# Sigmoid gates of two branches computed beside their branch products, with eight places for the attention heads' outputs

## What is computed

```
xn   = rms_norm(x, norm1_g)
proj = xn @ w_in        # q/k/v of mixers A, B, C and gate_pre (3 x 1024 columns)
o_a = dilated window attention (3 groups, 6 heads)      # width 384
o_b = bidirectional mLSTM (4 heads)                      # width 512
o_c = differential attention (4 heads), rms norm per head  # width 512
gates = sigmoid(gate_pre)                                # (3, 1024) per token
mixed = gates0 * (o_a @ w_a) + gates1 * (o_b @ w_b) + gates2 * (o_c @ w_c)
x = x + mixed @ w_out
x = x + (silu(hg) * hu) @ w_ffn_out,  hg, hu = split(rms_norm(x, norm2_g) @ w_ffn_in)
```

## Time and profile before

| | us |
|---|---|
| median of 3 runs | 3378.49 (3377.2 to 3378.5) |
| the profiled execution | 3374.39 |
| its span, first to last instruction | 3372.8 |
| PE busy in the span | 3162.7 |
| DVE, ACT, POOL busy | 1559.9, 1172.6, 511.2 |
| mean granted TensorE clock | 0.983 |

### The profile page before, as it was taken

One profiled execution on the slowest core, in us unless ns is written; L12 is line 12 of the kernel. 1 busy time (PEld: TensorE's weight loads), 2 busy tenths in 40 slices (PEclk: granted clock), 3 DMA queues, 4 the chain that ended last, 5 costly groups with the idle time before them and its releaser, 6 DMA issues. The chain is left out here.

```text
span 3372.8 us, 45846 instructions
## 1 busy us (share of the span) xinstructions
PE 3162.7 (94%) x17652; PEld 2898.3 (86%) x17652; DVE 1559.9 (46%) x3181; ACT 1172.6 (35%) x2496; POOL 511.2 (15%) x879
## 2 busy tenths in 40 slices
PE   6899999899999999999988999999999999999998
PEld 6899988788787999999878998887887889999997
DVE  5445235654465343443464442457544653433433
ACT  4334434465532211111143344344655322111110
POOL 1111322122152000000001113212212510000000
PEclk9999999999999999999989999999999999999999
DMA  3434443443275221221133344434433842212211
GB/s 129 142 113 122 137 136 122 127 125 118 86 210 169 63 74 39 75 71 41 32 127 121 98 136 131 145 109 131 124 112 95 215 148 63 75 50 62 75 47 60
DMA packets 273321, 358.63 MB, mean 106 GB/s; under 512 B 27377, under 2 KB 209841, under 8 KB 273129
## 3 DMA queue, kind: packets, MB, share of 16 engines
q1 hardware_dynamic: 213576, 179.41, 18.1%
q0 software_dynamic: 59552, 176.68, 16.6%
HBM read 264.42 MB, written 91.59 MB: 106 GB/s over the span
## 5 line engine op out<-in xcount | busy, mean ns | idle before, releaser
L1809 PE MATMUL ps<-wh,xh 128*128 128x384 f32 (+1 forms) x1440 | 536.9, 373 | 12.5 <-DVE wl L1409 6.7
L1811 PE MATMUL ps<-wh,xl 128*128 128x384 f32 (+1 forms) x1440 | 520.9, 362 | 0.0
L1810 PE MATMUL ps<-wl,xh 128*128 128x384 f32 (+1 forms) x1440 | 520.7, 362 | 0.0
L1809 PE MATMUL ps<-xh,wh 128*128 128x384 f32 (+1 forms) x1312 | 458.6, 350 | 17.2 <-DVE stage L1488 7.3
L1810 PE MATMUL ps<-xl,wh 128*128 128x384 f32 (+1 forms) x1312 | 442.1, 337 | 0.0
L1811 PE MATMUL ps<-xh,wl 128*128 128x384 f32 (+1 forms) x1312 | 442.1, 337 | 0.0
L1409 DVE TENSOR_TENSOR wl<-wraw,wh 128x1024 fp32r<-128x1024 f32 (+2 forms) x210 | 232.5, 1112 | 449.7 <-ACT wh L1127 449.3
L1883 PE MATMUL ps<-xh,wh 128*128 128x384 f32 x1280 | 326.6, 335 | 15.4 <-DVE arena L1796 15.4
L1883 PE MATMUL ps<-xl,wh 128*128 128x384 f32 x1280 | 324.7, 334 | 0.0
L1883 PE MATMUL ps<-xh,wl 128*128 128x384 f32 x1280 | 324.7, 334 | 0.0
L1809 PEld LDWEIGHTS ps<-wh,xh 128*128 128x128 f32 x1440 | 276.4, 192 | 42.3 <-DVE wl L1409 6.9
(11 more groups left out here) (229 smaller groups left out, 4980.7 us busy)
## 6 DMA issues: line engine op xcount, KB each, us to landing
wraw<-in_w_in SPq DMA_DIRECT2D x96, 512.0 KB, 3.8
wraw<-in_w_ffn_in SPq DMA_DIRECT2D x88, 512.0 KB, 4.0
wraw<-in_w_in SPq DMA_DIRECT2D x72, 384.0 KB, 3.4
wraw<-in_w_ffn_out SPq DMA_DIRECT2D x44, 512.0 KB, 3.4
qkv_a<-stage POOLq DMA_DIRECT2D x108, 192.0 KB, 2.2
gate_t<-stage POOLq DMA_DIRECT2D x96, 192.0 KB, 2.2
stage<-gate_t POOLq DMA_DIRECT2D x78, 192.0 KB, 4.2
mix_t<-stage POOLq DMA_DIRECT2D x52, 192.0 KB, 4.3
```

Of the source, the lines that this page charges most:

```text
L1809: pe.matmul(out, ah, bh, start=first, stop=False)
L1810: pe.matmul(out, ah, bl, start=False, stop=False)
L1811: return pe.matmul(out, al, bh, start=False, stop=last)
```

## The change

- `CHUNKS`: the gates of branch 2 take the place of those of branch 0 early on. The weights of branches 0 and 1 come in eight chunks "mix", each with two gate subs and one branch sub. The halves of `w_out` come in the other order, and `WOUT` with them.
- Dense order: for branches 0 and 1, gate i is followed by job i - 2. The six turns of branch 1 stand in two groups of three behind the first two gates of branch 1, and go to `oh`/`ol` in place of `xh`/`xl`. `GAP_C` is 3.7 in place of 4.
- A gate of branch 0 or 1 stays in its slot of `stage`. DVE multiplies the job into it, and POOL stores the slot to `mix_t`; it is free for the gate three later when that has landed. `gate_t` holds only branch 2.
- `c_o` has eight places; the flips have four banks, come after the last gate, in groups, and after `c_norm` of the last head. `c_norm` puts its squares into PSUM.
- `gated` (five) and `part_mix` (five in place of three) have places of their own. The first five gates of branch 2 are loaded at the last `c_norm`, up to five partial sums as they come. The tiles of x are loaded in the first six jobs of branch 2, with a semaphore for each three.

```diff
-PSLOTS = 3
+PSLOTS = 5
...
+    for b in range(2):
+        for i in range(4):
+            chunks.append(("mix", [gate(b, 2 * i), gate(b, 2 * i + 1), ("branch", *MIX_ROWS[b], 2 * i * P, 2 * P)]))
...
-GAP_A, GAP_B, GAP_C, ROUND = 4, (4, 4, 8), 4, 0.45
+GAP_A, GAP_B, GAP_C, ROUND = 4, (4, 4, 8), 3.7, 0.45
...
-    if kind == "c_norm" and s[1] >= 4:
-        return ("c_flip", s[1] - 4)
...
-    dense += [("gate", 0, d, q) for d in range(KD) for q in range(2)]
+    dense += [("gate", 2, d, q) for d in range(KD) for q in range(2)]
     dense += [("piece", c, t) for c in range(C_C, C_C + 3) for t in range(NT)]
-    dense += [("gate", b, d, q) for b in (1, 2) for d in range(KD) for q in range(2)]
-    for d in range(KD):
-        dense += [("branch", 0, d, q) for q in range(2)]
-        if d < NT:
-            dense.append(("turn", 1, d))
-        if d + 2 < NT:
-            dense.append(("turn_load", 1, d + 2))
-    dense += [("branch", 1, d, q) for d in range(KD) for q in range(2)]
+    jobs = [(d, q) for d in range(KD) for q in range(2)]
+    for b in range(2):
+        for i in range(len(jobs) + 2):
+            if i < len(jobs):
+                dense.append(("gate", b, *jobs[i]))
+                if b == 1 and i < 2:
+                    for t in range(3 * i, 3 * i + 3):
+                        dense.append(("turn", 1, t))
+                        if t + 2 < NT:
+                            dense.append(("turn_load", 1, t + 2))
+            if i >= 2:
+                dense.append(("branch", b, *jobs[i - 2]))
     dense += [("branch", 2, d, q) for q in (1, 0) for d in range(KD)]
...
-        if flips and flips[0] in normed and ("gate", 2, KD - 1, 1) in gone and (
+        if flips and flips[0] in normed and ("gate", 1, KD - 1, 1) in gone and ("c_norm", 7) in gone and (
...
-            flipped = spent
+            if flips and flips[0] % 3 == 0:
+                flipped = spent
...
                     def store_staged(step):
                         m = STAGE[step]
+                        if step[0] == "gate" and step[1] < 2:
+                            return
...
+                    def first_gates():
+
+                        stage_stored(STAGE["gate", 2, KD - 1, 1])
+                        pool.wait_ge(c_tr, len(C_FOLDS))
+                        pool.wait_ge(c_ptr, len(C_UNITS))
+                        pool.wait_ge(c_pv, len(C_UNITS))
+                        for j in range(GSLOTS):
+                            load_gate(j)
...
                     def mix(step):
                         _, b, d, q = step
                         i = MIXES[step]
+                        pool.wait_ge(mixed, i + 1)
                         if b < 2:
+                            m = STAGE["gate", b, d, q]
                             if b:
+                                stage_stored(STAGE["gate", 0, d, q])
                             add = {"accum_op": ALU.add} if b else {}
+                            pool.dma_start(mix_t[d * P:(d + 1) * P, HALVES[q]], stage[:, m % SLOTS, 0:HALF_TOK], **add
+                                           ).then_inc(stored[m % SLOTS], 16)
+                            if b and STEPS.index(("c_norm", 7)) < STEPS.index(step):
+                                first_parts(i - 2 * KD - 2)
                             return
                         j = i - MIX_LAST
+                        if j == 0:
+                            first_parts(2 * KD)
+                            pool.wait_ge(c_flo, len(C_HEADS))
+                        if j + PSLOTS < 2 * KD:
+                            load_part(j + PSLOTS)
+                        if 1 <= j and j - 1 + GSLOTS < 2 * KD:
+                            load_gate(j - 1 + GSLOTS)
+                        if j < NT:
+                            t = FFN_TILES[j]
+                            pool.dma_start(x[:, t, :], x_save[t * P:(t + 1) * P, :]).then_inc(x_back[j // 3], 16)
...
                             if H and t == 0:
-                                pe.wait_ge(c_ov, H)
+                                pe.wait_ge(co_ss, H)
...
                             pe.wait_ge(co_n, H + 1)
-                            flip_bank_free(pe, step)
+                            if H == 0:
+                                pe.wait_ge(c_ex, 2 * len(C_UNITS))
+                                pe.wait_ge(c_pt, len(C_UNITS))
+                                pe.wait_ge(co_ss, len(C_HEADS))
+                            if H >= 4:
+                                pe.wait_ge(c_flo, H - 3)
```

More of the change, by code:

```diff
@@ L76, in chunk_list @@
         chunks.append(("bvo", [("in", 2 * j, 2, COL_B + i * B_W, B_W) for j in range(4)]))
-    gates = [("gate", [("in", 0, 8, COL_GATE + (4 * i + j) * P, P) for j in range(4)]) for i in range(6)]
-    chunks += gates[0:2]
+    gate = lambda b, d: ("in", 0, 8, COL_GATE + (KD * b + d) * P, P)
+    for i in range(2):
+        chunks.append(("gate", [gate(2, 4 * i + j) for j in range(4)]))
     for i in range(3):
         chunks.append(("c", [("in", 2 * j, 2, COL_C + i * C_W, C_W) for j in range(4)]))
[L81 to L85, removed]
+    for b in range(2):
+        for i in range(4):
+            chunks.append(("mix", [gate(b, 2 * i), gate(b, 2 * i + 1), ("branch", *MIX_ROWS[b], 2 * i * P, 2 * P)]))
+    chunks.append(("branch", [("branch", *MIX_ROWS[2], 2 * j * P, 2 * P) for j in range(4)]))
+    for h in (1, 0):
         chunks.append(("out", [("wout", 2 * j, 2, h * 512, 512) for j in range(4)]))
@@ L472, in build @@
         nmx_d = dram("nmx_d", (2, B_H, TOK))
[L473 removed]
+        gate_t = dram("gate_t", (D, TOK))
         mix_t = dram("mix_t", (D, TOK))
@@ L550, in build, with at @@
         g_zero = area("bg", 4 * P)
[L552 to L565, removed]
+        def at(first, n):
+            assert first + n <= arena_floats
+            return arena[:, first:first + n]
+        c_v = at(early, 2 * 4 * P).rearrange("p (r t n) -> p r t n", r=2, t=4)
+        c_qt = at(early + 1024, 2 * 4 * P).rearrange("p (r n) -> p r n", r=2)
+        c_kt = at(early + 2048, 2 * 4 * P).rearrange("p (r n) -> p r n", r=2)
+        first_o = [512 * h for h in range(4)] + [2048, 2304, early + 3072, 10240]
+        assert 2560 <= early and early + 3072 + 256 <= NT * D
+        c_o = [at(first_o[H], SEQS[s_][1] * P).rearrange("p (t n) -> p t n", n=P) for H, (s_, h) in enumerate(C_HEADS)]
+        c_e = at(NT * D, 2 * 2 * 4 * P).rearrange("p (r m n) -> p r m n", r=2, m=2)
+        c_at = at(NT * D + 2048, 2 * 4 * P).rearrange("p (r n) -> p r n", r=2)
+        c_in = at(NT * D + 3072, 2 * 4 * P).rearrange("p (i t n) -> p i t n", i=2, t=4)
+        gated = [at(NT * D + i * HALF_TOK, HALF_TOK) for i in range(GSLOTS)]
+        part_mix = [at(NT * D + (GSLOTS + i) * HALF_TOK, HALF_TOK) for i in range(PSLOTS)]
+        assert NT * D + (GSLOTS + PSLOTS) * HALF_TOK <= 10240
         turn_in = wide[:, :].rearrange("p (r n) -> p r n", r=2)
@@ L671, in build, with flip_bank @@
         AT_TURN, AT_OUT, AT_FOLD = 1024, 1536, 2048
[L673 to L679, removed]
+        def flip_bank(H):
+            return side[:, 512 * (H % 4):512 * (H % 4 + 1)]
         def mix_rows(hi, d):
@@ L855, in store_staged, with load_gate @@
                         pool.dma_start(dst, src).then_inc(stored[m % SLOTS], 16)
[L856 to L859, removed]
+                    def load_gate(j):
+                        _, b, d, q = MIX_LIST[MIX_LAST + j]
+                        if j >= GSLOTS:
+                            pool.wait_ge(r_lo, j - GSLOTS + 1)
+                        pool.dma_start(gated[j % GSLOTS], gate_t[d * P:(d + 1) * P, HALVES[q]]).then_inc(gate_in[j % GSLOTS], 16)
@@ L1101, in _ @@
                                 load_cv(C_LAST.index(step[1]) + 2)
+                        elif kind == "c_norm" and step[1] + 1 == len(C_HEADS):
+                            first_gates()
                         elif kind == "turn_load":
                             load_turn(*step[1:])
+                        elif kind == "turn" and step[1:] == (1, NT - 1):
+                            pool.wait_ge(d_done, INDEX["turn", 1, NT - 1] + 1)
+                            pool.dma_start(wide[:, :], io["norm2_g"][layer].partition_broadcast(P)
+                                           ).then_inc(gain2_in, 16)
                     for sem_, total in [(a_loaded[i], loads[i]) for i in range(3)] + [
```

149 lines of the change are left out of this document (59 added, 90 removed).

## The result

| | before | after |
|---|---|---|
| median of 4 runs | 3378.49 us | 3440.85 us (3439.5 to 3443.14) |
| profiled execution, its span | 3374.4, 3372.8 us | 3439.93, 3438.3 us |
| mean granted clock of TensorE | 0.983 | 0.971 |

The ratio is 1.0186, with a 95% interval of 1.0168 to 1.0203: slower by 62 us, outside the range that was given (3346 to 3410). The forecast was no change.

A forecast was written before the change was run, and what follows sets the result against it. TensorE, 94% busy, plus its waits bounds the kernel. Per layer attention 20.5 us replaces 15.6, flips +3, branch 2 jobs -8.3, clock +1.7: +1.3, +2.6 for two layers, giving 3381 us (no change), range 3346 to 3410.

The forecast's parts named there:

- Clock: TensorE at 1.2 instead of 2.4 GHz for a stretch after a long wait: 1.7 us per layer, bounds 0 and 8.5.
- every wait above 2.5 us drops the clock: Slower rival: five waits per layer cost 1.7 us of clock each instead of one, +6.8 per layer, 3395 us; chance 0.07.
- The first three slots, beside the jobs of branch 0, lose about 2.: Start of the attention stage: TensorE loses about 2 us per layer in the first three attention slots.
- The rival of the ring: Slower rival: ACT's copies of gates (1,1,1) to (1,7,1) wait for staging slots, +12 us per layer, 3405; chance 0.17.
- Splits followed by a job: Attention stage: scores wait where a split-carrying gate is followed by a short job, 2.8 us three times, then 2.0.
- The last two splits: Attention stage, gates (1,5,0) and (1,5,1): their weight splits cost 0.5 us together, since scores end there.
- Turns: Branch 1: the third turn of each group waits for its load from o_tok, 3.6 us twice, 7.2 per layer.
- Flips: Grouped among branch 1's last jobs, they load ACT and VectorE; job (2,0,1) needs four: 3 us, bounds 0 and 6.
- Jobs of branch 2: Sixteen jobs with earlier loads of gates and partial sums: 1.5 us of waits remain instead of 9.8, gain 8.3 per layer.
- The faster rival: Attention stage: ACT and VectorE reach slots early, so short filler does not show; -10 us per layer, 3361; chance 0.30.
- the waits of the third and sixth turn: Sign in branch 1: these two turns each wait 3 to 4 us for wide from o_tok.
- None above 1 us elsewhere: Sign in the attention stage: scores wait near 2.8 us behind gates with splits, and nowhere else above 1 us.

The follow-up runs named there:

- Products in the waits: Changed kernel with 292 matrix products without a use, placed before the steps where TensorE waits: 3421.17 us, ratio to before 1.0125.
- mended pairs: Changed kernel with branch 1's six turns in three pairs, the first ahead of gate (1,0,0), a gate between the last pair and job (1,0,0): 3425.17 us.
- the last version: Changed kernel with splits on the jobs, turns in pairs before gates, loads of wide behind score 1, and late loads of x: 3365.79 us, ratio 0.9960.

## Why the prediction was wrong

By its own steps, per layer, in layer 0:

- **Clock: the step that failed by most.** It was taken at 1.7 us, one wait's worth, with 8.5 as the bound. Products in the waits gave back 32 us of busy time, 16 a layer, twice the bound. The term was sized on two waits of before, of which the one of 2.9 us had cost nothing, and so waits of about 3 us were counted as free. In after the 24 us behind the 7.92 us wait have a granted clock of 0.86, where the earlier trace rows had 0.93. The rival "every wait above 2.5 us drops the clock" named the mechanism, and had 0.07 and half the price; its threshold is not borne out, as the rows behind 2.33 and 1.84 us show.
- **"The first three slots, beside the jobs of branch 0, lose about 2."** They lost 11.6: score 1 with 7.9, and 0.4 to 1.6 at four other steps. The working looked at the engines and not at POOL's queue, where the loads of wide now stand ahead of a store on which the staging ring waits. The rival of the ring had the right resource and the wrong place: it set a flat 1 us at each of twelve gates of branch 1, and the stall was one, in branch 0, made by a neighbour in the queue. With the loads moved 3.7 us of it went, and with splits and turns moved too 7.2.
- **Splits followed by a job: right.** 2.8, 2.8, 2.8 and 2.0 were predicted, and 3.13, 2.69, 3.13 and 2.33 measured, by a chain of 7.68 us, which moving the splits took away. The prediction's own terms, 7.68 less a slot of 2.37 and a job of 2.1, give 3.2. The last two splits, put at 0.5 "since scores end there", cost 3.57. That of gate (1,5,0) also lies ahead of turn 22 (L2044), which waits for ACT's copy of the turn before (L1330), and this copy stands behind the last exponentials.
- **Turns: right in sum.** 3.6 twice predicted, 3.00 and 4.77 measured, and gone once in mended pairs. Why the second is longer was not followed.
- **Flips: about right.** 3 predicted, 3.5 measured: 1.68 at a flip, and 1.82 before job (2,0,1), for which the trace names no releaser. That job needs four flips, and DVE writes the fourth (L1744) from 1048.20, just before the job begins at 1048.98.
- **Jobs of branch 2: right in kind.** Predicted to gain 8.3 and lose 1.5 to waits; the stage went from 43.5 to 36.7 and lost 2.3. Late loads of x brought it to 33.8, the 33.6 of the sum.
- **The faster rival**, in which the short filler doesn't show, held 0.30. It asked that VectorE and ScalarE run ahead of a serial chain; they did not.
- **Signs and range.** Of the signs named, the waits of the third and sixth turn came, and no transpose of q and k waited for a flip. "None above 1 us elsewhere" failed by the 7.92 at score 1, and ScalarE was seen waiting for stores of mix_t, which the prediction took as a sign of being wrong. The lower end of the range, 3346, doesn't follow from its own terms: 3381 less 20 (the faster rival), 3.4 (the clock) and 3 (the jobs at their bound) is 3355.

The sum gave an idle time almost unchanged and 1.7 us of clock. Measured are 17.4 us of idle time and 15.4 of busy time a layer. Of the idle part 9.6 are the first slots and 3.1 the turn of slot 22. Both large errors are of one kind: a wait was priced by the engines' own chain, without the clock behind it and without the queue beside it.

## What to carry to other kernels

When an order alternates long and short filler between the steps of a serial chain, put what isn't part of the chain (here the weight splits, 2.3 us over two engines) on the short filler, behind the chain's next step, and not ahead of it. Price additional idle time of the engine that bounds the kernel at about twice its length until the granted clock says otherwise, as two rows cannot give that price. As a sum it came out so here (17.4 us idle, 15.4 busy a layer). Wait by wait it did not: shortening the longest from 7.92 to 4.23 us gave back idle time only, so take waits away whole, or put work into them. For each step that is moved, read the queue that issues its transfers: what stands behind a waiting load waits too, and here a ring of three slots carried that to ScalarE and on to TensorE.

## What the runs showed of the hardware

That 292 more products can make a kernel 20 us faster was not expected, nor that the same products a step later cost 49. In the region of after the granted clock was 0.93, with no wait above 8 us in it, and it fell behind waits of 2.33 and, in the last version, 1.84 us, while one of 1.97 us in before and one of 2.33 with the loads of wide moved left it at 1.00. The DMA engines' share fell from 0.56 to 0.41 in that region, and the load of wide took a median of 3.1 us from issue to landing instead of 3.9; the time rose all the same.
